# Streamed tensors 64 bytes behind a multiple of 128, and the low weight parts divided between VectorE and GpSimd by stage

## The reference

```python
# block 1, per layer
u = rms_norm(h, norm_mix_g[layer]);  p = u @ w_in[layer]
ys = jnp.stack([y_a, y_b, y_c], axis=2)          # rwkv7, hgrn2 and sparse attention, from p
branch = jnp.einsum('bsnc,ncd->bsnd', ys, w_branch[layer])
merged = jnp.sum(jax.nn.sigmoid(gates) * branch, axis=2)
h = h + merged @ w_o[layer]
h = h + conv_glu(rms_norm(h, norm_ffn_g[layer]), w_up[layer], conv_w[layer], conv_b[layer], w_down[layer])
# block 2, per layer
x = x + mix @ w_out                               # mlstm, moba and latent attention, from rms_norm(x) @ w_in
x = x + jnp.square(jax.nn.relu(rms_norm_2(x, g_mlp_norm) @ w_up)) @ w_down
```

## Time and profile before

| | |
|---|---|
| median of three runs | 2285.23 us (2284.57 to 2291.86) |
| span of the profiled execution | 2285.6 us |
| PE, busy | 2026.4 us (89%) |
| POOL, busy | 1405.5 us (61%), in 1008 subtractions |
| DVE, busy | 1192.3 us (52%) |
| ACT, busy | 1152.7 us (50%) |
| mean granted clock of TensorE | 0.925 |

### The profile page before, as it was taken

How to read it: one execution, slowest core, us unless ns; L and a number is a source line. 1 busy time by engine, 2 the same in 40 slices (tenths; PEclk the granted TensorE clock), 3 DMA queues, 4 the chain that set the end, 5 groups by cost and what they waited for, 6 DMA issues and landing times.

```text
span 2285.6 us, 44204 instructions
## 1 busy us (share of the span) xinstructions
PE 2026.4 (89%) x14950; PEld 1910.6 (84%) x14950; DVE 1192.3 (52%) x1649; ACT 1152.7 (50%) x1928; POOL 1405.5 (61%) x1012
## 2 busy tenths in 40 slices
PE   5898898989997999888998997789889989878998
PEld 5888787989997889787998997776789978668998
DVE  2366765247932365775346952277666015765620
ACT  3634235446654654235446653564554446564543
POOL 4672015878986673005887985563389966417996
PEclk8999799999998999799999998897899989789999
DMA  5442003555664542002555664331256644204664
GB/s 166 131 117 67 1 1 94 165 148 159 185 182 126 144 121 77 19 1 65 159 164 144 184 181 140 92 107 56 72 146 184 188 131 134 74 24 139 173 192 144
DMA packets 146627, 274.12 MB, mean 120 GB/s; under 512 B 16273, under 2 KB 16274, under 8 KB 146194
## 3 DMA queue, kind: packets, MB, share of 16 engines
q1 hardware_dynamic: 145584, 267.32, 41.3%
q10 hardware_dynamic: 866, 4.31, 0.5%
HBM read 270.52 MB, written 1.05 MB: 119 GB/s over the span
## 4 chain that ended last, share of the span: by engine, by line
issue 49%; POOL 40%; PE 10%; POOLq 1%; DVE 0%; ACT 0%; ACTq 0%
POOL ring_split L575 40%; PE bank L585 10%; POOLq L572 1%; POOLq L569 0%; ACT arena L1158 0%; POOLq L575 0%; DVE u L1679 0%; DVE arena L1664 0%; ACT rn L1158 0%; DVE u_split L1684 0%; DVE arena L1665 0%; DVE rn L1665 0%; ACTq L245 0%; ACTq L253 0%; POOLq L2279 0%
## 5 line engine op out<-in xcount | busy, mean ns | idle before, releaser
L575 POOL TENSOR_TENSOR ring_split<-ring,hi_ring 128x512 fp32r<-128x512 f32 x1008 | 1405.3, 1413 | 866.9 <-ACT hi_ring L1158 834.4
L1158 ACT ACTIVATE hi_ring<-ring 128x512 fp32r<-128x512 f32 x1008 | 621.9, 630 | 599.3 <-PE bank L585 567.2
L585 PE MATMUL bank<-u_hi,hi_ring 128*128 128x256 f32 (+1 forms) x2480 | 734.4, 296 | 112.2 <-POOL ring_split L575 76.8
L585 PE MATMUL bank<-u_split,hi_ring 128*128 128x256 f32 (+1 forms) x2480 | 715.9, 289 | 0.0
L585 PE MATMUL bank<-u_hi,ring_split 128*128 128x256 f32 (+1 forms) x2480 | 714.9, 288 | 0.0
L585 PEld LDWEIGHTS bank<-u_hi,hi_ring 128*128 128x128 f32 (+1 forms) x2480 | 485.4, 196 | 137.2 <-POOL ring_split L575 95.6
L585 PEld LDWEIGHTS bank<-u_split,hi_ring 128*128 128x128 f32 (+1 forms) x2480 | 487.2, 196 | 1.5
L585 PEld LDWEIGHTS bank<-u_hi,ring_split 128*128 128x128 f32 (+1 forms) x2480 | 486.7, 196 | 1.0
L585 PE MATMUL bank<-arena 128*128 128x128 f32 (+5 forms) x2368 | 343.4, 319 | 31.4 <-ACTq L253 6.6
L585 PEld LDWEIGHTS bank<-arena 128*128 128x128 f32 (+2 forms) x2368 | 308.8, 206 | 70.0 <-issue 31.9
L1158 ACT ACTIVATE arena<-bank 128x512 f32<-128x512 f32 (+4 forms) x262 | 135.9, 519 | 281.5 <-PE bank L585 243.9
(11 more groups left out here) (236 smaller groups left out, 2347.3 us busy)
## 6 DMA issues: line engine op xcount, KB each, us to landing
ring<-in_stream SPq DMA_DIRECT2D x1008, 256.0 KB, 2.8
par<-in_params ACTq DMA_DIRECT2D x5, 637.0 KB, 5.0
h<-in_x SPq DMA_DIRECT2D x1, 1024.0 KB
out<-h ACTq DMA_DIRECT2D x1, 1024.0 KB, 3.9
cst<-in_cst SPq DMA_DIRECT2D x1, 962.0 KB
arena<-in_masks SPq DMA_DIRECT2D x1, 960.0 KB
arena<-in_positions ACTq DMA_DIRECT2D x1, 1.0 KB
```

Of the source, the lines that this page charges most:

```text
L575: nc.gpsimd.tensor_tensor(ring_lo[:, c, o:o + PIECE * P], x_, hi_ring[:, i % HI_RING, :].bitcast(F32), ALU.subtract).then_inc(pieces_split, 1)
L585: ins = nc.tensor.matmul(o, l, r, start=start, stop=stop)
L1158: return nc.scalar.activation(o, i, f, **kw)
```

## The change

The first edit concerns addresses. A tensor `phase` of 64 bytes is put behind `hi_ring`, and another fill ahead of the arena, so that u, u_hi and the arena start 64 bytes behind a multiple of 128; `Carve` rounds each start up to 32 words. The second concerns the low parts. `Owners` decides per piece, by the name that it belongs to, which engine makes the low part. In block 1 DVE makes those of A1 to A6, of the merge but for G0, G1 and M0 in the order of the stream, and of WO, U and D; in block 2 those of cq1 to ak, of the second half of WO, of U and of D. POOL makes the others. `LoParts` is DVE's counterpart of `HiParts`, with a call ahead of DVE's wait for the bank of each name; where DVE has the pieces of cq1 to ak of block 2 there is one call for all of them. PE waits for one of two semaphores, by the owner of the piece.

```diff
@@ -98,6 +98,19 @@
               ("rot", P), ("rotp", P), ("rotd", P), ("cos", T), ("sin", T), ("freq", 2),
               ("eps", 1), ("gn_eps", 1))
 MERGE = tuple((f"G{j}{n}", f"M{j}{n}", n, j) for n in BRANCHES for j in range(4))
+BY_VECTOR1 = {f"A{i}" for i in range(1, 7)} | {m[0] for m in MERGE[2:]} | {m[1] for m in MERGE[1:]}
+BY_VECTOR1 |= {f"WO{j}" for j in range(4)} | {f"U{i}" for i in range(22)} | {f"D{j}" for j in range(4)}
+BY_VECTOR2 = {"cq1", "ckv", "kpe", "aq", "ak"} | {f"WO{j}" for j in range(4)} | {f"U{i}" for i in range(16)} | {f"D{j}" for j in range(4)}
+SIZES1 = [(f"A{i}", 16) for i in range(7)] + [(n, 16) for n in ("Bq0", "Bq1", "Bf0", "Bf1", "Cq0", "Cq1", "Ck")]
+SIZES1 += [("Bi0", 32), ("Cqi", 16), ("Cki", 8), ("Cv", 16), ("Bg0", 16), ("Bg1", 16), (MERGE[0][0], 16)]
+for i in range(len(MERGE)):
+    SIZES1 += [(m[0], 16) for m in MERGE[i + 1:i + 2]] + [(MERGE[i][1], 8)]
+SIZES1 += [(f"WO{j}", 16) for j in range(4)] + [(f"U{i}", 16) for i in range(22)] + [(f"D{j}", 44) for j in range(4)] + [("end", 8)]
+SIZES2 = [("cq0", 16), ("cq1", 8), ("ckv", 16), ("kpe", 8)] + [(n, 16) for n in ("aq", "ak", "av", "qk0", "qk1")]
+SIZES2 += [("uq0", 6), ("uq1", 6), ("uk0", 2), ("uk1", 2), ("uv", 4), ("if", 8), ("mv0", 32), ("mo0", 16), ("mo1", 16)]
+SIZES2 += [(f"WO{j} attention", 8) for j in range(4)] + [(f"WO{j}", 8) for j in range(4)]
+SIZES2 += [(f"U{i}", 16) for i in range(16)] + [(f"D{j}", 64) for j in range(4)] + [("end", 4)]
+assert sum(n for _, n in SIZES1) == BLOCKS1 and sum(n for _, n in SIZES2) == BLOCKS2
 MASKS = Columns(("up", LEVELS * P), ("low", LEVELS * P), ("diag", P))
@@ -253,19 +266,37 @@
         eng.sem_inc(self.free[self.slot[name][0]], 1)
+class Owners:
+
+
+    def __init__(self, sizes, by_vector, pieces):
+        self.by_vector, at = [False] * pieces, 0
+        for name, n in sizes:
+            for p in range(-(-at // PIECE), -(-(at + n) // PIECE)):
+                self.by_vector[p] = name in by_vector
+            at += n
+        self.total = {v: self.by_vector.count(v) for v in (False, True)}
+
+    def count(self, p):
+
+        return self.by_vector[:p + 1].count(self.by_vector[p])
+
+
 class Weights:
-    def __init__(self, pe, lo_ring, hi_ring, split, used, first, ends):
-        self.pe, self.lo_ring, self.hi_ring, self.split, self.used, self.first = pe, lo_ring, hi_ring, split, used, first
+    def __init__(self, pe, lo_ring, hi_ring, owners, made, used, ends):
+        self.pe, self.lo_ring, self.hi_ring, self.owners, self.made, self.used = pe, lo_ring, hi_ring, owners, made, used
         self.ends, self.seen, self.next, self.pending, self.told = ends, 0, 0, 0, 0
+        self.sizes = {}
     def take(self, name, n):
         q = self.next
         self.next += n
         self.ends[name] = -(-self.next // PIECE)
+        self.sizes[name] = self.sizes.get(name, 0) + n
         return q
     def block(self, q, n=1):
@@ -273,7 +304,8 @@
         p, at = q // PIECE, q % PIECE * P
         assert q % PIECE + n <= PIECE
         if p >= self.seen:
-            self.pe.wait_ge(self.split, self.first + (p + 1))
+            made, first = self.made[self.owners.by_vector[p]]
+            self.pe.wait_ge(made, first + self.owners.count(p))
             self.seen = p + 1
         c, o = q // CHUNK % RING, q % CHUNK * P
         return (self.hi_ring[:, p % HI_RING, at:at + n * P], self.lo_ring[:, c, o:o + n * P])
@@ -384,6 +417,7 @@
         ring, ring_lo = with_twin("ring", [P, RING, CHUNK * P])
         h = sb("h", [P, KD, T])
         hi_ring = sb("hi_ring", [P, HI_RING, PIECE * P], F32R)
+        sb("phase", [P, 16])
         u, u_lo = with_twin("u", [P, KD, T])
         u_hi = sb("u_hi", [P, KD, T], F32R)
         par = sb("par", [P, PAR_SIZE])
@@ -391,8 +425,10 @@
         cst = sb("cst", [P, CST.size])
         msk = sb("msk", [P, MASKS.size], U8)
         small = sb("small", [P, 128])
-        ARENA = 36192
-        arena_at = -(-nc.sbuf_base // 32) * 32
+        sb("arena_phase", [P, (64 - nc.sbuf_base) % 128 // 4])
+        ARENA = 36416
+        arena_at = nc.sbuf_base
+        assert arena_at % 128 == 64
         arena = sb("arena", [P, ARENA])
         banks = [ctx.enter_context(nc.psum_tensor(f"bank{i}", [P, 512], F32)) for i in range(8)]
@@ -401,8 +437,8 @@
                 self.at = start
             def __call__(self, n):
-                a = self.at
-                self.at += n
+                a = -(-self.at // 32) * 32
+                self.at = a + n
                 assert self.at <= ARENA, self.at
                 return arena[:, a:a + n]
@@ -564,15 +601,16 @@
         @block.gpsimd
         def _(pool):
-            n = (layers[0] * CH1 + layers[1] * CH2) // RING
-            per_round = RING * CHUNK // PIECE
-            with pool.Fori(0, n) as r:
-                for i in range(per_round):
-
-                    pool.wait_ge(hi_written, r * per_round + (i + 1))
-                    c, o = i * PIECE // CHUNK, i * PIECE % CHUNK * P
-                    x_ = ring[:, c, o:o + PIECE * P]
-                    nc.gpsimd.tensor_tensor(ring_lo[:, c, o:o + PIECE * P], x_, hi_ring[:, i % HI_RING, :].bitcast(F32), ALU.subtract).then_inc(pieces_split, 1)
+            for n, own, before in ((layers[0], own1, 0), (layers[1], own2, layers[0] * PIECES1)):
+                if not n:
+                    continue
+                with pool.Fori(0, n) as l:
+                    for q, by_vector in enumerate(own.by_vector):
+                        if by_vector:
+                            continue
+                        pool.wait_ge(hi_written, l * len(own.by_vector) + (before + q + 1))
+                        c = q % RING
+                        nc.gpsimd.tensor_tensor(ring_lo[:, c, :], ring[:, c, :], hi_ring[:, q % HI_RING, :].bitcast(F32), ALU.subtract).then_inc(lo_by_pool, 1)
         @block.tensor
@@ -1690,6 +1731,23 @@
                 C.link(V.tensor_tensor(x_, x_, spread(cos, n), ALU.mult))
                 C.link(V.tensor_tensor(x_, x_, t, ALU.add))
+            class LoParts:
+
+
+                def __init__(self, ends, own, first):
+                    self.ends, self.own, self.first, self.at = ends, own, first, 0
+
+                def upto(self, name, lead=LEAD):
+
+                    stop = min(self.ends[name] + lead, max(self.ends.values()))
+                    for q in range(self.at, stop):
+                        if not self.own.by_vector[q]:
+                            continue
+                        dve.wait_ge(hi_written, self.first + (q + 1))
+                        c = q % RING
+                        V.tensor_tensor(ring_lo[:, c, :], ring[:, c, :], hi_ring[:, q % HI_RING, :].bitcast(F32), ALU.subtract).then_inc(lo_by_vector, 1)
+                    self.at = max(self.at, stop)
+
             dve.wait_ge(inputs_in, 48)
             C = Chain(dve, ready)
             C.link(V.tensor_copy(msk[:], mask_in))
@@ -1707,6 +1766,7 @@
                 norm_parts(C, p("g_mix"), rn[:], 0)
                 for i in range(14):
+                    lo.upto(f"A{i // 2}")
                     dve.wait_ge(S["pmu_ready"], 2 * (i // 2) + 2)
                     bank = B.wait(dve, f"A{i // 2}")
                     C.link(V.scalar_tensor_tensor(pa[:, i, :], bank[:, i % 2 * T:(i % 2 + 1) * T], omu[:, i:i + 1],
...
@@ -2015,6 +2076,7 @@
                     if last:
                         split(C, o, merged_hi[:, j * 512:(j + 1) * 512], merged_lo[:, j * 512:(j + 1) * 512], S["merged_ready"])
                 for j in range(4):
+                    lo.upto(f"WO{j}")
                     bank = B.wait(dve, f"WO{j}")
                     o = h[:, 2 * j:2 * j + 2, :].rearrange("p a t -> p (a t)")
                     C.link(V.tensor_tensor(o, o, bank[:, :], ALU.add), S["h_ready"])
...
@@ -2024,6 +2086,7 @@
                 for i in range(23):
                     if i < 22:
+                        lo.upto(f"U{i}")
                         bank = B.wait(dve, f"U{i}")
                         dve.wait_ge(S["conv_in"], i + 1)
                         for d, w_, sig in ((1, "conv_w1", None), (2, "conv_w0", S["conv_mid"])):
...
@@ -2226,11 +2293,13 @@
                 refine(C, "mlp", 7)
                 norm_parts(C, p("g_mlp"), dn, KD // 2)
                 for i in range(16):
+                    lo.upto(f"U{i}")
                     dve.wait_ge(S["conv_in"], 4 + i + 1)
                     x_ = hidden[:, 2 * i:2 * i + 2, :].rearrange("p a t -> p (a t)")
                     C.link(V.tensor_tensor(x_, x_, x_, ALU.mult))
                     split(C, x_, hidden_hi[:, 2 * i:2 * i + 2, :].rearrange("p a t -> p (a t)"), hidden_lo[:, 2 * i:2 * i + 2, :].rearrange("p a t -> p (a t)"), S["hidden_ready"])
                 for j in range(4):
+                    lo.upto(f"D{j}")
                     bank = B.wait(dve, f"D{j}")
                     o = h[:, 2 * j:2 * j + 2, :].rearrange("p a t -> p (a t)")
```

(10 more changed lines are left out.)

5 lines of the change are left out of this document (4 added, 1 removed).

## The result

| | before | after |
|---|---|---|
| median | 2286.82 us (2284.57 to 2291.86) | 2313.82 us (2312.34 to 2314.86) |
| profiled span | 2285.6 us | 2311.6 us |

The changed kernel takes 1.0111 times the time of before, 95% interval 1.0095 to 1.0126. The forecast was 2268, with a range up to 2300: wrong in size and in sign.

The account below looks back on a forecast made before the run. PE was taken to bound the kernel, with POOL at nearly the same pace and DVE interwoven. Block 1 +16.8 and block 2 -33.8 sum to -17.0, from 2285.23 to 2268 us; own range 2246 to 2287, wider range 2238 to 2300.

Parts of the forecast that it names:

- block 1, A to merge: Block 1 before WO: A -2.0, middle projections -1.5, merge -1.3 us per layer, from closer matmuls and shorter DVE instructions.
- WO: Block 1's WO: last merged part ready 3.8 us earlier and 2.2 of slow clock spared, -6.0 us per layer.
- up: Block 1's up: PE waits 1.40 us for DVE's piece in each of 22 projections, +22.4 us per layer.
- down: Down stages: block 1 -3.2 us per layer by an earlier start and closer matmuls; block 2 -4.5 per layer.
- block 2, up: Block 2's up: DVE's piece is ready in time, no PE wait; 90.6 us against 98.8, -8.2 per layer.
- front, middle and WO: Block 2: front and middle -2.2 us by closer matmuls, WO -2 by shorter DVE instructions, per layer.
- the price of the first edit: Matmuls on u, hidden and branch outputs would take merged's spacing, 113.3 ns; 51 us lie between 120 and 113.3.
- rival 1: All matmuls concerned: the start address does nothing and the spacing has another reason; 2319 us, chance 0.08.
- 2, DVE not late: Block 1's up: DVE's own work is shorter than read, so the stage takes 123.3 us; kernel 2210, chance 0.08.
- 3, a part of the spacing: Matmul spacing gains only in part, half-way between the forecast and rival 1; 2294 us, chance 0.10.
- 4, the slow clock in "up": Block 1's up: PE's stands lower the clock, a projection takes 10.2 us; 2411 if it lasts, chance 0.04.

Follow-up runs that it names:

- e1: The kernel before with only the address edit of the change; 2270.57 us, ratio 0.9929 to before.
- e15: The changed kernel with u and the arena 64 bytes behind a multiple of 256; 2297.02 us, ratio 1.0028 to before.
- e2: The changed kernel without the address edit, so only the low parts are divided anew; 2324.05 us, ratio 1.0169 to before.
- e4: The changed kernel with DVE making one piece earlier, right behind the multiply-adds of block 1's up projections; 2269.96 us, ratio 0.9918 to before.
- e3: The changed kernel with the pieces of block 1's up stage given back to POOL; 2257.18 us, ratio 0.9872 to before.
- e9: The kernel of e3 once more, unchanged, for a second profile; no median time is given.
- e7: e3 with ScalarE writing the high parts of Bq0's last piece ahead of two table loads; 2242.21 us, ratio 0.9788 to before.
- e18: e7 plus two merge edits, weights at a multiple of 256 bytes, u and the arena 192 behind one; 2220.98 us, ratio 0.9715 to before.

## Why the prediction was wrong

Per layer, from the starts and ends of the stages:

| term | forecast, us | measured, first layer | second layer |
|---|---|---|---|
| block 1, A to merge | -4.8 | +0.9 | +5.5 |
| WO | -6.0 | -2.0 | -2.0 |
| up | +22.4 | +24.6 | +24.6 |
| down | -3.2 | -0.5 | -0.7 |
| block 2, up | -8.2 | -6.0 | -7.1 |
| down | -4.5 | -0.6 | -0.3 |
| front, middle and WO | -4.2 | -5.3 | -4.6 |

The three changes from one layer to the next come to -0.4, -1.4 and +0.9.

**The step that failed: the price of the first edit.** "I price it at the spacing of merged, 113.3 ns" read a spacing off another tensor and put it down to the start modulo 128. Merged's start had one more property, 192 bytes (mod 256) from the weights, and the edit left u at 64. The 51 us that the prediction set on the address were 17 alone (e1) and 10 beside the split. Even with merged's distance (e15) they would have been 27 beside the split, 2324.05 - 2297.02 (32 by the ratios), with 59% of the matmuls on u at the short spacing. Of the error of 46 us 41 lie here, 51 less 10. The prediction named the weak point ("the spacing was compared between tensors and not on one"), and gave the case 0.08: rival 1's 2319 is 5 us from the result. e2, the split at the old spacing, is at 2324, 5 us above the same rival: the other terms were right in sum. In part that was luck: per layer e2 takes 25 us more than the kernel before in block 1, for the 21 of that rival, and 7 less in block 2, for its 4. A hint lay in the kernel before as well: the high part of a branch output starts 64 bytes behind a multiple of 128 as merged does, with its low part elsewhere, and its matmuls lie 118 to 119 ns apart.

The Trainium skill ("TensorE: Matmul & The Clock Gate", Back-to-back issue gap) gives the isolated gap of warm matmuls by the number of columns alone, and has both the weight loads and the matmuls set the spacing in a stream of them; an operand's start has no part in either. It spoke against the change, and rightly for the outcome, but the runs don't bear it out as a rule for this stream: at 256 columns one operand runs at 113 or 118 ns, and at 120 from another start.

**Right.** PE waits once in every projection of block 1's "up", for DVE's piece. The latency was put at 5.48 us behind the start of the next projection and is 604.33 - 598.80 = 5.53. The period was put at 6.84 and is 7.05, the stage at 152.7 and is 154.9: the last piece takes 1.52 us and not 1.36, 0.05 of it by the spacing and 0.10 by the first step behind the stand, which takes 0.22 us for 0.12. The period less 48 x 0.1177 leaves 1.40 lost per projection, the forecast's number, but of another make: 1.29 of waiting and 0.10 of that first step. e4 shows that the latency makes the wait, e3 that this stage alone carries more than the whole loss: without it the change is 1.3% faster than before. Also right were block 2's "up" without a wait; DVE's cast at 0.29 and 0.43 with POOL at rest; PE idle from 375.8 to 388.8 in the merge (375.5 to 389.2).

**Mis-sized.** WO: "the part is ready at 480.3", and it is ready at 483.5. Of these 3.2 us 2.3 are the merge's, which ends at 478.3 and was put at 476.0 with its matmuls at 113.3. The rest is DVE's own new work, which the forecast left out: it makes two low parts for the next name ahead of the last product. PE waits 2.3 us for the part, 4.1 before:

```profile
479.55 1.29 DVE L1748 TENSOR_TENSOR ring_split<-ring,hi_ring 128x512 fp32r<-128x512 f32 x2
480.75 0.68 DVE L2072 TENSOR_TENSOR arena<-bank,arena 128x512 f32<-128x512 f32 x1
...
482.78 0.69 DVE L1699 TENSOR_TENSOR merged_lo<-arena,merged_hi 128x512 fp32r<-128x512 f32 x1
```

The front of block 1 has a term that I had put at nothing: PE's stand before Bq0's last piece, and the clock behind it. PE works again at 81.31 us, 82.26 before, but the 24 fp32 matmuls that follow ran at 0.50 nearly to their end in the changed kernel, and at 1.00 for the most part in the kernel before. These matmuls in the kernel before, in the changed one, and in the two layers of e9:

```profile
85.01 5.26 PE L585 MATMUL bank<-arena,par 64*128 64x256 f32 x24
```

```profile
83.57 9.12 PE L623 MATMUL bank<-arena,par 64*128 64x256 f32 x24
```

```profile
83.71 9.18 PE L623 MATMUL bank<-arena,par 64*128 64x256 f32 x24
...
778.31 5.04 PE L623 MATMUL bank<-arena,par 64*128 64x256 f32 x24
```

That is 3.9 us per layer in the profiled executions. It isn't shown to be the change's doing: e9 has both lengths in one execution, behind the same stand of 3.5 us. What decides between them stays open. e7 shows the stand itself to be the cause of the slow clock. I had not looked at what stands between A and the middle.

**The rivals.** 2, DVE not late, fell. 3, a part of the spacing, is what e1 shows as a mechanism, but with 2 of 6.7 ns, not half. 4, the slow clock in "up", didn't come: it was 0.99 there.

## What to carry to other kernels

A duration that differs between two tensors belongs to no single property of theirs until one tensor has been moved alone; one run with only the address edit would have shown this. When an engine that works in program order takes over a part of another's stream, price the latency from the event that PE makes to the part that PE needs, and put that part right behind the instructions that release a buffer: here the same work cost 44 us in one place and not in the other. The best version, e18 (POOL for block 1's "up", one high part early, the merge, and streamed operands 192 bytes from the weights, modulo 256), takes 2221 us, 67 less than the kernel before beside it (2288.41).

## What the runs showed of the hardware

Matmuls of 256 columns at the full clock came in two kinds: 113 ns apart, or some 117 to 120 by the start of the streamed operand, mostly 117.7. A run nearly always keeps its kind from one break to the next, and which one it takes differs between executions of the same program. The share of the short kind follows the distance between the streamed operand and the weights modulo 256 bytes: on u over half at 192, at most 16% elsewhere; on hidden 50 to 74% at 192, at most 24% elsewhere. That holds for streams against the ring's weights. Where the ring is streamed and u is the weight, at 512 columns, distance 192 in the changed kernel was the slower one (236 ns for 227 at 0). What draws the kind stays open, and so does the spread of merged at 192: 95% short before, 92 after, 27 and 94 in the two profiles of e3's kernel, 50 to 71 where u stands at 192 too. It makes 3.3 us per up stage of block 2, and so bears on how far two profiles of one kernel may differ: for a few us, medians of several executions are wanted.

A stand of TensorE of 3.4 to 3.7 us before Bq0's last piece was followed by a granted clock of 0.50 in every kernel that has it, and how long the slow clock lasted differed between the two layers of one execution in e9 (24 fp32 matmuls in 9.18 and in 5.04 us).
